# Second attention of a transformer block: scores from stacked high and low key parts in two fp32r passes, in place of a full fp32 product over zero-masked queries

## What is computed

```python
def _gqa_attention(gq, gk, gv):                     # 8 query heads of 64, 2 key heads, 4 query heads each
    s = jnp.einsum('bqhgd,bkhd->bhgqk', gq, gk).astype(jnp.float32) * ATTN_SCALE
    p = jax.nn.softmax(s, axis=-1).astype(gv.dtype)
    return jnp.einsum('bhgqk,bkhd->bqhgd', p, gv)
```

## Time and profile before

| | us |
|---|---|
| median of 3 runs (lowest, highest) | 4083.15 (4079.98, 4084.63) |
| the profiled execution: its time | 4075.62 |
| its span, from the first to the last instruction | 4073.8 |
| TensorE busy | 3853.2 (95%) |
| VectorE (DVE) busy | 2133.5 (52%) |
| GpSimd (POOL) busy | 1484.0 (36%) |
| ScalarE (ACT) busy | 1346.3 (33%) |
| mean granted TensorE clock | 0.980 of full speed |

### The profile page before, as it was taken

The page is one execution under the profiler, slowest core; times in us unless marked ns, Lnnn a source line. Parts: engine busy times, 40 slices in busy tenths (PEclk is TensorE's granted clock), DMA queues, the critical chain, the costliest instruction groups (busy, mean ns, idle before and its releaser), DMA issues.

```text
span 4073.8 us, 48594 instructions
## 1 busy us (share of the span) xinstructions
PE 3853.2 (95%) x18340; PEld 3096.0 (76%) x18340; DVE 2133.5 (52%) x2959; ACT 1346.3 (33%) x1779; POOL 1484.0 (36%) x1012
## 2 busy tenths in 40 slices
PE   8999898999998989999999899999798999999999
PEld 7888775877886848757888778888675757777887
DVE  5555846036776361457732357777644348624334
ACT  3222644242224242352232332222424252334223
POOL 3555341436663202103433224444221305544443
PEclk9999999999999999999999999999899999999999
DMA  5554221224442101101122123333110202222222
GB/s 216 185 188 174 75 94 39 103 81 154 157 155 85 56 1 52 47 1 49 66 73 73 52 104 124 124 124 124 48 52 21 78 1 83 93 103 75 95 98 83
DMA packets 57650, 367.28 MB, mean 90 GB/s; under 512 B 5792, under 2 KB 12192, under 8 KB 14112
## 3 DMA queue, kind: packets, MB, share of 16 engines
q1 hardware_dynamic: 42064, 271.11, 19.1%
q10 hardware_dynamic: 15440, 94.12, 6.2%
HBM read 363.11 MB, written 2.10 MB: 90 GB/s over the span
## 4 chain that ended last, share of the span: by engine, by line
issue 62%; POOL 28%; PE 9%; POOLq 0%; DVE 0%; ACT 0%; DVEq 0%; ACTq 0%
POOL b_wlo L602 28%; PE ps L1768 3%; PE ps L1770 3%; PE ps L1769 3%; POOLq L616 0%; DVE b_y L1260 0%; POOLq L618 0%; DVE b_x L1264 0%; DVE b_y L1317 0%; PE ps L1844 0%; ACT b_whi L643 0%; PE ps L1831 0%; ACT b_xout L709 0%; DVE b_small L1262 0%; POOLq L602 0%
## 5 line engine op out<-in xcount | busy, mean ns | idle before, releaser
L602 POOL TENSOR_TENSOR b_wlo<-b_raw,b_whi 128x512 fp32r<-128x512 f32 x1008 | 1483.8, 1504 | 2569.3 <-ACT b_whi L643 2569.3
L1768 PE MATMUL ps<-b_hhi,b_whi 128*128 128x512 f32 x3032 | 1118.4, 369 | 21.1 <-POOL b_wlo L602 12.8
L1769 PE MATMUL ps<-b_hlo,b_whi 128*128 128x512 f32 x3032 | 1108.9, 366 | 0.0
L1770 PE MATMUL ps<-b_hhi,b_wlo 128*128 128x512 f32 x3032 | 1108.3, 366 | 0.0
L643 ACT ACTIVATE b_whi<-b_raw 128x2048 fp32r<-128x2048 f32 x252 | 481.5, 1911 | 902.1 <-PE ps L1770 877.5
L1768 PEld LDWEIGHTS ps<-b_hhi,b_whi 128*128 128x128 f32 x3032 | 573.2, 189 | 126.1 <-issue 22.7
L1769 PEld LDWEIGHTS ps<-b_hlo,b_whi 128*128 128x128 f32 x3032 | 573.6, 189 | 93.3 <-issue 1.9
L1770 PEld LDWEIGHTS ps<-b_hhi,b_wlo 128*128 128x128 f32 x3032 | 573.0, 189 | 93.0
L1317 DVE TENSOR_TENSOR b_y<-ps,b_y 128x512 f32<-128x512 f32 x496 | 335.6, 689 | 242.0 <-PE ps L1770 242.0
L1768 PE MATMUL ps<-b_whi,b_dhi 128*128 128x512 f32 x992 | 393.6, 397 | 0.1
L1770 PE MATMUL ps<-b_whi,b_dlo 128*128 128x512 f32 x992 | 393.4, 397 | 0.0
(11 more groups left out here) (306 smaller groups left out, 4674.7 us busy)
## 6 DMA issues: line engine op xcount, KB each, us to landing
b_raw<-panels SPq DMA_DIRECT2D x252, 1024.0 KB, 4.7
b_mraw<-mod_panels ACTq DMA_DIRECT2D x78, 1024.0 KB, 4.9
b_y<-mod_panels ACTq DMA_DIRECT2D x3, 1024.0 KB, 15.8
b_xin<-xT SPq DMA_DIRECT2D x1, 2048.0 KB, 25.4
b_mraw<-mod_panels SPq DMA_DIRECT2D x2, 1024.0 KB, 17.1
b_crow<-par ACTq DMA_DIRECT2D x2, 1024.0 KB, 5.1
b_rope<-rope ACTq DMA_DIRECT2D x4, 512.0 KB, 3.5
outT<-b_xout SPq DMA_DIRECT2D x4, 512.0 KB, 3.6
```

Of the source, the lines that this page charges most:

```text
L602: ins = pool.tensor_tensor(wlo[:, s, c], raw[:, s, c], whi[:, s, c].bitcast(F32), ALU.subtract)
L1768: pe.matmul(out, a[0], b[0], start=first, stop=False)
L1769: pe.matmul(out, a[0], b[1], start=False, stop=False)
L1770: return pe.matmul(out, a[1], b[0], start=False, stop=last)
```

## The change

The scores of the g attention become two single-pass fp32r products per stretch of keys. The key tile of a head is stacked: its high part in the 64 rows of that head, its low part in the other 64 (`ks`, one plane for each of the two key heads). The queries of a unit are stored as two planes of 128 rows, the high part twice and the low part twice (`qs0`, `qs1`, in turn by unit). High part times the stack and low part times the stack are summed in PSUM.

These parts have to be made. ACT writes the high parts (`query_hi`, two copies of 64 by 512 or 256, at the step that is five rows ahead of the unit, behind row_exp), DVE the low parts (`query_lo`, two instructions, three rows ahead, in front of row_probs), in place of the one masked query on DVE. The keys are split once for each layer (`key_hi`, `key_lo`). Keys are now projected, normed and rotated first, the last query tile's rotation comes in front of the attention, and the transposes of the values move behind the first two scores. Some buffers get other places.

```diff
-    ps += cols_panels(w[:, 2176:2688][:, PAIRED], 0, 512) + cols_panels(w, 1024, 1280)
+    ps += cols_panels(np.concatenate([w[:, 1024:1152], w[:, 2176:2688][:, PAIRED], w[:, 1152:1280]], axis=1), 0, 3 * CW)
...
+    def first_row(self, n):
+        return [row[0] for row in self.rows].index(n)
+    def last_row(self, n):
+        return max(r for r, row in enumerate(self.rows) if row[0] == n)
+    def units_at(self, r, ahead):
+        return [n for n in range(1, len(self.units)) if max(self.first_row(n) - ahead, -1) == r]
...
+            qs0 = sb("qs0", [2, L], F32R, s2)
...
-    DV_BANK, GK_BANK = [4, 5, 6, 7, 4, 5], 2
-    GV_BANK = {TT: 6, L: 0}
-    GQ_BANK = {TT: [0, 2, 6, 0], L: [0, 1, 6, 7]}
+    DV_BANK = [4, 5, 6, 7, 4, 5]
+    GQ_BANK = {TT: [2, 6, 0, 2], L: [2, 3, 6, 7]}
+    GK_BANK, GV_BANK = 0, {TT: 6, L: 0}
...
-    HEAD_TAGS = [("gq", 0), ("gq", 1), ("gq", 2), ("gq", 3), ("gk", 0)]
+    HEAD_TAGS = [("gk", 0), ("gq", 0), ("gq", 1), ("gq", 2), ("gq", 3)]
     head_no = HEAD_TAGS.index
+    head_size = lambda tag, T: TT if tag[0] == "gk" else T
+    head_bank2 = lambda tag, T: GK_BANK if tag[0] == "gk" else GQ_BANK[T][tag[1]]
+    query_split = lambda v: (qs0, qs1)[v % 2]
+    own_rows = lambda half: slice(64 * half, 64 * half + 64)
...
+            def query_hi(rows, v):
+                t, half, g = rows.unit(v)
+                a, b = GROUPS[g]
+                o = own_rows(half)
+                act.wait_ge(*at(*rows.query_event(X, t, g)))
+                if v == 1:
+                    act.wait_ge(*at("roped", X("gq", 3)))
+                if v >= 2:
+                    act.wait_ge(*at("scores", X("g", rows.last_row(v - 2), rows.unit(v - 2)[1])))
+                act.activation(query_split(v)[o, 0, 0:b - a], aq[o, t, a:b], ACT.Copy, scale=SCALE).then_inc(*up("c_hi", X("q own", v)))
+                act.activation(query_split(v)[own_rows(1 - half), 0, 0:b - a], aq[o, t, a:b], ACT.Copy, scale=SCALE)\
+                   .then_inc(*up("c_hi", X("q", v)))
+            def key_hi():
+                act.wait_ge(*at("roped", X("gk", 0)))
+                for half in range(2):
+                    o = own_rows(half)
+                    act.activation(ks[o, half, :], gk[o, 0, :], ACT.Copy).then_inc(*up("c_hi", X("k", half)))
+            def keep_values():
+                act.wait_ge(*at("v_turned", X()))
+                act.activation(gv[:, :, :], wide(4, TT).rearrange("p (t n) -> p t n", n=P), ACT.Copy).then_inc(*up("gv", X()))
             def attention(rows):
+                if rows.tag == "g":
+                    keep_values()
+                    for v in rows.units_at(-1, 5):
+                        query_hi(rows, v)
...
+                    for v in rows.units_at(r, 5) if rows.tag == "g" else ():
+                        query_hi(rows, v)
...
-            def squares_of(t):
-                head_squares(("gq", t), GQ_BANK[T][t], T, ("out", (pq + t // 2, t % 2)))
-            def norm_head(tag, size):
+            rows = ROWS(st, "g")
+            next_split()
+            for i, tag in enumerate(HEAD_TAGS):
+                size = head_size(tag, T)
+                head_squares(tag, head_bank2(tag, T), size, ("out", (pq + i // 2, i % 2)))
+                if i in (1, 3):
+                    next_split()
+                if i == 2:
+                    key_hi()
+                if i == 4:
+                    query_hi(rows, 0)
                 head_root(tag, size)
                 keep_rows(tag, size)
-            for a in range(2):
-                if a == 0:
-                    next_split()
-                squares_of(2 * a)
-                norm_head(("gq", 2 * a), T)
-                squares_of(2 * a + 1)
-                next_split()
-                norm_head(("gq", 2 * a + 1), T)
-            head_squares(("gk", 0), GK_BANK, TT, ("out", (pq + 2, 0)))
-            norm_head(("gk", 0), TT)
             act.wait_ge(*at("out", (pq + 2, 1)))
-            act.activation(pr2[:, 1, 0, :], wide(GV_BANK[T], TT), ACT.Copy).then_inc(*up("v_kept", X()))
-            act.wait_ge(*at("v_turned", X()))
-            act.activation(gv[:, :, :], wide(4, TT).rearrange("p (t n) -> p t n", n=P), ACT.Copy).then_inc(*up("gv", X()))
-            rows = ROWS(st, "g")
+            act.wait_ge(*at("roped", X("gq", 2)))
+            act.activation(pr2[:, 0, 1, :], wide(GV_BANK[T], TT), ACT.Copy).then_inc(*up("v_kept", X()))
             attention(rows)
...
+            def query_lo(rows, v):
+                t, half, g = rows.unit(v)
+                a, b = GROUPS[g]
+                o = own_rows(half)
+                dve.wait_ge(*at("c_hi", X("q", v)))
+                src, hi = aq[o, t, a:b], query_split(v)[o, 0, 0:b - a].bitcast(F32)
+                dve.scalar_tensor_tensor(query_split(v)[o, 1, 0:b - a], src, SCALE, hi, ALU.mult, ALU.subtract)
+                dve.scalar_tensor_tensor(query_split(v)[own_rows(1 - half), 1, 0:b - a], src, SCALE, hi, ALU.mult, ALU.subtract)\
+                   .then_inc(*up("qm", X("g", v, half)))
...
-                    for q, j in steps:
+                    for q, j in steps if rows.tag == "d" else ():
                         if rows.unit_start(q):
                             masked_query(rows, q, j)
+                    for v in rows.units_at(r, 3) if rows.tag == "g" else ():
+                        query_lo(rows, v)
                     row_probs(rows, r)
...
-            for t in range(4):
-                head_reciprocal(("gq", t), T)
-                if t:
-                    turn("gq", t - 1, aq[:, t - 1, 0:L], aq[:, t - 1, 0:L], pr2[:, t % 2, 1, 0:L], "rope2")
-                normed(("gq", t), T, GQ_BANK[T][t], pcol("q_norm", l), aq[:, t, 0:T])
-                dve.wait_ge(*at("hnormed", X(("gq", t))))
-            turn("gq", 3, aq[:, 3, 0:L], aq[:, 3, 0:L], pr2[:, 0, 1, 0:L], "rope2")
-            for t in range(4):
-                dve.wait_ge(*at("roped", X("gq", t)))
-            first_queries(ROWS(st, "g"))
-            head_reciprocal(("gk", 0), TT)
-            normed(("gk", 0), TT, GK_BANK, pcol("k_norm", l), gk[:, 0, :])
-            dve.wait_ge(*at("hnormed", X(("gk", 0))))
-            turn("gk", 0, gk[:, 0, 0:L], gk[:, 0, 0:L], pr2[:, 1, 1, 0:L], "rope2")
-            attention(ROWS(st, "g"))
+            gq_rows = ROWS(st, "g")
+            head_tile = lambda tag: gk[:, 0, :] if tag[0] == "gk" else aq[:, tag[1], :]
+            def turn_head(i):
+                tag = HEAD_TAGS[i]
+                turn(*tag, head_tile(tag)[:, 0:L], head_tile(tag)[:, 0:L], pr2[:, (i + 1) % 2, 1, 0:L], "rope2")
+            def key_lo():
+                for half in range(2):
+                    o = own_rows(half)
+                    dve.wait_ge(*at("c_hi", X("k", half)))
+                    dve.tensor_tensor(ks[own_rows(1 - half), half, :], gk[o, 0, :], ks[o, half, :].bitcast(F32), ALU.subtract)\
+                       .then_inc(*up("c_lo", X("k", half)))
+            for i, tag in enumerate(HEAD_TAGS):
+                size = head_size(tag, T)
+                head_reciprocal(tag, size)
+                if i:
+                    turn_head(i - 1)
+                if i == 3:
+                    key_lo()
+                normed(tag, size, head_bank2(tag, T), pcol("k_norm" if tag[0] == "gk" else "q_norm", l), head_tile(tag)[:, 0:size])
+                dve.wait_ge(*at("hnormed", X(tag)))
+            query_lo(gq_rows, 0)
+            turn_head(4)
+            attention(gq_rows)
...
+                size = T[n] if isinstance(T, list) else T
...
+            def split_scores(rows, r, j):
+                u, i, js, k0, k1 = rows[r]
+                if rows.unit_start(r):
+                    pe.wait_ge(*at("qm", X("g", rows.unit_no(r), j)))
+                if r == 0:
+                    pe.wait_ge(*at("c_lo", X("k", 1)))
+                b = rows.bank(r, j)
+                claim([b, b + 1] if k1 - k0 > L else [b], ("exp", X("g", r, j)))
+                q = query_split(rows.unit_no(r))[:, :, (i % 4) * P:(i % 4 + 1) * P]
+                for n, (c0, c1) in enumerate([(k0, L), (L, k1)] if k0 == 0 else [(k0, k1)]):
+                    for part in range(2):
+                        ins = pe.matmul(ps[:, b + n, 0:c1 - c0], q[:, part, :], ks[:, j, c0:c1], start=(part == 0), stop=(part == 1))
+                ins.then_inc(*up("scores", X("g", r, j)))
...
-            def attention(rows, keys, values):
+            def turn_values():
+                pe.wait_ge(*at("v_kept", X()))
+                claim([4, 5], ("gv", X()))
+                for t in range(6):
+                    ins = pe.transpose(ps[:, 4 + t // 4, (t % 4) * P:(t % 4 + 1) * P], pr2[:, 0, 1, t * P:(t + 1) * P], const("ident"))
+                ins.then_inc(*up("v_turned", X()))
+            def attention(rows, scores, values):
                 for step in rows.first_steps():
-                    row_scores(rows, *step, keys)
+                    scores(rows, *step)
+                if rows.tag == "g":
```

(51 more changed lines are left out.)

## The result

Over twenty runs of each on the same chips the changed kernel takes 4087.8 us (4080.5 to 4093.6) and the kernel before 4078.7 (4072.9 to 4084.6): the ratio is 1.0022, 95% interval 1.0015 to 1.0029, 9.1 us more. (The kernel before lies 4.5 us under the three runs that were known ahead.) The profiled execution took 4083.1 us, its span 4081.3; before it was 4075.6 and 4073.8.

The account below looks back on a forecast made before the run. TensorE, busy 95% of the span, was taken as the bound. Minus 8.3 (mix3), minus 0.5 (heads), plus 10.0 (mix2) and plus 9.1 (clock) gave plus 10.3 us, 4093 against the median; range 4075 to 4103.

Parts of the forecast that it names:

- the hold in mix2: Ahead of a wide unit's fourth transposes TensorE waits 3.1 us for parts and probabilities; pair 19.0 against 17.58, plus 10.0.
- the falls of the clock: In mix2, TensorE's clock drops at each of seven waits of 3.1 us; 1.3 us each, plus 9.1 us.
- a shorter unit in mix3: A unit of four rows in mix3's g attention takes 12.76 us for 14.15; six full units gain 8.3.
- the heads: Reordered norms, rotations and projections ahead of the attention: a gain of 0.5 us in all, between 0 and 2.
- The 44 us: TensorE time saved on score products over 64 wide and 32 narrow rows, 38 + 6; said not to count by itself.
- the rival of TensorE alone: Both g attentions: TensorE is the only bound, so all 44 us and 10 of waits go; 4029 us, chance 0.04.
- the ring: mix3: a row's transposes wait for the previous row's copy, one pair of banks; 1.86 us a turn, taken as 1.88.
- The cover of the parts: mix3: ACT and DVE write high and low parts while resting during the 5.2 us values product, so they cost nothing.
- the 2.6 named as the most for both: mix3: up to 2.6 us a unit if the values product no longer hid the high and low parts.
- the rows of 2.99 and 2.41: Two waits in the earlier trace: behind 2.99 us the clock was 0.50, behind 2.41 between dense products it stayed 1.00.
- Without this hold the pair would gain 1.0: mix2: were the fourth transposes not held up, they would start at 9.5 and a wide-narrow pair would gain 1.0 us.
- the parts hide: mix2, ahead of the fourth row's probabilities: parts take under 1.2 us instead of 2.6, so faster, 4067 us; chance 0.13.

Follow-up runs that it names:

- the wait filled: Changed kernel with three products that nobody reads issued ahead of the fourth transposes in mix2: 4078.6 us, ratio 1.0000 to the kernel before.
- the three runs without the hold: Changed kernel with mix2's low parts two rows ahead (run twice, 0.9987 and 0.9983) or high parts six rows ahead (0.9986), ratios to the kernel before.
- the third pass: Changed kernel with three fp32r passes per score product instead of two, in both stages: 4094.0 us, ratio 1.0043 to the kernel before.

## Why the prediction was right

The forecast was plus 10.3 us, 4093 against a median of 4083; it came out plus 9.1, against a median that proved to be 4079. So it was slower by 0.22%, at 4088, inside the range. Whether that is beyond the 0.2% is not clear: the interval is 0.15 to 0.29%. The mechanism was right, the hold in mix2 with the falls of the clock against a shorter unit in mix3. The closeness of the sum is partly luck. mix3 was taken as minus 8.3 and its stage gained 11.5; mix2 with the clock was taken as plus 19.1 and its stage lost 20.6; the heads were taken as a gain of 0.5 that is not seen. Errors of 3.2 one way and 2.0 the other leave 1.2.

- **The products.** The 44 us count 32 narrow rows where mix2 has 16; it is 38 + 3 = 41. It is not what counts: with 24 of the 41 us given back, 7.6 show. Nothing else in the sum hangs on it; the rival of TensorE alone would have been 3 us higher.
- **mix3.** 12.76 a unit was forecast, 12.54 measured: minus 1.61 instead of 1.39. A row goes from transposes to transposes in 1.81 to 1.84 us, not 1.88 (1.89 at a unit's last row). The timeline agrees with the ring: transposes 0.85, 0.03 to the copy, copy 0.81, 0.15 back, 1.84 in all. (The 0.14 back stands in none of the rows named; in the kernel before it can be read in mix2, a copy's end at 1718.39 and the transposes at 1718.53.) The cover of the parts was right between units: 1.4 us more of them cost nothing a unit, and the low parts two rows ahead cost 1.16 a unit. The high parts kept their cover in that run, so the 2.6 named as the most for both were not tested. Overlooked was the second unit, whose parts have no cover. And 1.7 of the stage's 11.5 us are the slow last product that the kernel before had and this one has not, which was in no term of the forecast.
- **mix2, the hold.** 19.0 us a pair without the clock was forecast; with the wait filled it is 19.0. The steps of the unit stood to within 0.2 us: from the end of the wide product at 1749.57, exp ends at 8.3 (8.4), high parts at 9.7 (9.5), low parts at 11.2 (11.0), transposes at 12.1 (11.9).
- **The clock.** 1.3 us a pair taken, 1.5 measured, at all seven. The argument for it was partly lucky. I weighed the length of the wait, 3.1 us against the rows of 2.99 and 2.41; but a rest of 2.1 brings the clock down too. And the slow time was to run out partly in the wait; it does in two of the seven units, in the other five the clock falls behind the wait. The price of 1.3 was a choice of half between two ends, and it came out near. The Trainium skill ("TensorE: Matmul & The Clock Gate", section "HAM oscillation — how this bites in real kernels") says that waits between bursts of products throttle the array again each time. The seven falls agree with it; the rests of 1.2 to 1.4 us behind two extra products, after which the clock stayed, show that it does not hold for every wait.
- **What was wrong in a step.** "Without this hold the pair would gain 1.0": it gains 0.25 (17.33) or 0.18 (17.40), and only while the clock is full. ACT's two high parts (1.26 us) hold up the copy of the third row, and the fourth transposes wait for it. So the rival "the parts hide" gives about 11 us by the stages, mix3's share, not 16, and 5 to 7 by the ratios of the three runs without the hold.
- **The heads.** 0.5 us forecast as a gain; in mix3 the first transposes do come 0.6 sooner, and the second unit's parts take it back (16.1 us both times). In mix2 the first values product comes 2.8 us later (17.8 after the stage's start for 14.9). The first unit's hold and fall are in this, and one fall more, in the first rows (transposes of 1.51 us at 1711.82), which was not forecast. Every kernel with the new scores in mix2 has slow transposes there, and the two with the old ones have none; without the hold the product is still 0.9 to 2.2 later.
- **TensorE as the only bound** falls with the third pass and with mix2, whose stage without the hold is as long as before.

Not tried: another pair of banks for the transposes in mix3, which would test the ring itself; the kernel uses all eight there. Until then the ring is read from the timeline and not shown by a run.

## What to carry to other kernels

Work that is moved off the bound engine comes back as preparation on the others, and in an in-order queue its place matters more than its length: the same two instructions of 0.69 us cost 1.2 us a unit more in mix3 at one row than at the row before it, and in mix2, the other way round, 1.7 us a pair more (19.0 against 17.33, both at full clock). A distance in rows that fits one stage need not fit another whose units alternate in size; look in the trace for the engine that idles in front of the preparation, and move either end. Look at the first unit too, where the cover that hides the preparation later may not be there yet. And price a wait of TensorE twice, once for its length and once for the slow products behind it; in mix2 they cost the same, 10.6 and 10.1 us. Where the rows are set by other engines, the fewer passes may be worth nothing: in mix2 the old scores were as fast as the best of the new ones.

## What the hardware showed that was not expected

- A rest of 2.07 to 2.22 us among light rows brought the clock down in all seven units (values product 6.83 us instead of 5.42), and ahead of two of the falls with high parts six ahead stood one of 1.53, while 2.41 between dense products did not the earlier trace rows; 1.21 or 1.35 us with two products ahead of it did not either.
- Products that nobody reads, put into a wait that is there anyway, brought back 10.1 us of 20.6; with one of them nothing came back, with two or three the whole share of the clock.
- Among rows with the new scores the clock fell with no wait over 0.8 us just ahead of it (the 1.52 at 1776.31), in one execution and not in another of the same kernel; the two stages differ by 6 us.
- A copy of 64 rows by 512 into fp32r took 0.63 us on ACT and the difference 0.69 on DVE, and 0.41 and 0.42 with 256 columns.
